# Exchanging the second and third of three matmuls per weight tile in a split-precision matrix product

## The reference, cut to what matters

```python
def sq_relu_mlp(h, w_in, w_out):
    return jnp.square(jax.nn.relu(h @ w_in)) @ w_out      # 2048 -> 8192 -> 2048

def conv_gated_mlp(h, w_up, conv_w, conv_b, w_down):
    up = h @ w_up                                          # 2048 -> 11264
    up = causal_depthwise_conv(up, conv_w) + conv_b
    gate, val = jnp.split(up, 2, axis=-1)
    return (jax.nn.silu(gate) * val) @ w_down              # 5632 -> 2048
```

## Time and profile before

| | |
|---|---|
| median of 3 runs | 2592.11 us (2591.83 to 2593.83) |
| the profiled execution | 2592.11 us, its span 2590.3 us |
| mean granted TensorE clock | 0.993 of full speed |
| TensorE matmul busy | 2537.2 us, 98% of the span |
| VectorE, ScalarE busy | 1658.1 us (64%), 1132.6 us (44%) |
| DMA | 547.89 MB, mean 212 GB/s |

### The profile page before, as it was taken

The page is one execution under the profiler, slowest core; times in us unless marked ns, Lnnn a source line. Parts: engine busy times, 40 slices in busy tenths (PEclk is TensorE's granted clock), DMA queues, the critical chain, the costliest instruction groups (busy, mean ns, idle before and its releaser), DMA issues.

```text
span 2590.3 us, 42561 instructions
## 1 busy us (share of the span) xinstructions
PE 2537.2 (98%) x18912; PEld 2378.3 (92%) x18912; DVE 1658.1 (64%) x1999; ACT 1132.6 (44%) x1299; POOL 11.2 (0%) x24
## 2 busy tenths in 40 slices
PE   6999999999999999999999999999999999999998
PEld 3688799999998999999999999999899889988996
DVE  5366666677785755555555579776677556764775
ACT  3322565544444434434434552054455435543553
POOL 0000000000000000000000000000000000000000
PEclk8999999999999999999999999999999999999999
DMA  9976565588885755555555555454455555555553
GB/s 395 361 254 229 209 218 207 202 296 290 304 292 202 278 190 186 194 192 185 194 193 184 190 183 179 147 179 170 151 185 196 196 194 187 188 195 184 190 183 110
DMA packets 77223, 547.89 MB, mean 212 GB/s; under 512 B 8848, under 2 KB 8976, under 8 KB 12272
## 3 DMA queue, kind: packets, MB, share of 16 engines
q1 hardware_dynamic: 74304, 533.53, 57.7%
q0 software_dynamic: 2448, 11.14, 1.1%
q10 hardware_dynamic: 288, 0.50, 0.1%
HBM read 539.90 MB, written 5.24 MB: 210 GB/s over the span
## 4 chain that ended last, share of the span: by engine, by line
PE 96%; DVE 2%; ACT 1%; DMA 1%; issue 0%; SPq 0%; DVEq 0%; ACTq 0%
PE acc L289 23%; PE acc L293 22%; PE acc L291 22%; PE acc L346 5%; PE acc L309 5%; PE acc L310 5%; PE acc L311 5%; PE mp L376 1%; PE mp L309 1%; PE mp L311 1%; PE mp L310 1%; DMA raw<-in_w_mod 1%; PE mp L435 0%; PE mp L498 0%; DVE macc L420 0%; PE mp L1866 0%
## 5 line engine op out<-in xcount | busy, mean ns | idle before, releaser
L257 DVE TENSOR_TENSOR wlo<-raw,whi 128x1024 fp32r<-128x1024 f32 x773 | 934.9, 1222 | 679.4 <-ACT whi L247 677.7
L247 ACT ACTIVATE whi<-raw 128x1024 fp32r<-128x1024 f32 x773 | 812.1, 1058 | 1171.9 <-PE acc L293 873.3
L293 PE MATMUL acc<-hl,whi 128*128 128x256 f32 x3296 | 922.6, 280 | 0.0
L289 PE MATMUL acc<-hh,whi 128*128 128x256 f32 x3296 | 919.4, 279 | 0.0
L291 PE MATMUL acc<-hh,wlo 128*128 128x256 f32 x3296 | 915.2, 278 | 0.0
L289 PEld LDWEIGHTS acc<-hh,whi 128*128 128x128 f32 x3296 | 622.5, 189 | 4.6 <-issue 3.0
L293 PEld LDWEIGHTS acc<-hl,whi 128*128 128x128 f32 x3296 | 618.8, 188 | 0.0
L291 PEld LDWEIGHTS acc<-hh,wlo 128*128 128x128 f32 x3296 | 616.7, 187 | 0.5
L293 PE MATMUL acc<-ml,whi 128*128 128x256 f32 x1536 | 430.1, 280 | 0.0
L289 PE MATMUL acc<-mh,whi 128*128 128x256 f32 x1536 | 426.4, 278 | 0.0
L291 PE MATMUL acc<-mh,wlo 128*128 128x256 f32 x1536 | 426.4, 278 | 0.0
(11 more groups left out here) (319 smaller groups left out, 2181.4 us busy)
## 6 DMA issues: line engine op xcount, KB each, us to landing
raw<-in_w_in SPq DMA_DIRECT2D x98, 1024.0 KB, 4.9
raw<-in_w_mod SPq DMA_DIRECT2D x96, 1024.0 KB, 5.8
raw<-in_w_up SPq DMA_DIRECT2D x88, 1024.0 KB, 4.9
raw<-in_w_mlp_in SPq DMA_DIRECT2D x64, 1024.0 KB, 4.9
raw<-in_w_mlp_out SPq DMA_DIRECT2D x64, 1024.0 KB, 4.9
raw<-in_w_down SPq DMA_DIRECT2D x44, 1024.0 KB, 4.9
raw<-in_w_out SPq DMA_DIRECT2D x32, 1024.0 KB, 4.9
raw<-in_w_fourier_out SPq DMA_DIRECT2D x8, 1024.0 KB, 5.7
```

The source lines that it names most:

```text
L247: nc.scalar.activation(whi[:, r, :], raw_slot(k)[:, 2 * GC * j:2 * GC * (j + 1)], ACT.Copy)\
L257: nc.vector.tensor_tensor(wlo[:, r, :], raw_slot(k)[:, 2 * GC * j:2 * GC * (j + 1)], whi[:, r, :].bitcast(f32), ALU.subtract).then_inc(S[" ...
L289: nc.tensor.matmul(dst, whi[:, r, cols], hi[:, kt, :], start=begin, stop=False, skip_group_check=True)
L293: last = nc.tensor.matmul(dst, whi[:, r, cols], lo[:, kt, :], start=False, stop=kt == nkt - 1, skip_group_check=True)
```

## The change

Within `feature_piece` the second and third matmul trade places. Before, the order is `whi` x high, `wlo` x high, `whi` x low; after it, `whi` x high, `whi` x low, `wlo` x high. The flag that closes the sum in PSUM and the increment of `used` stay with the third position. Operands, shapes, counts and waits are otherwise as before.

```diff
                     nc.tensor.matmul(dst, whi[:, r, cols], hi[:, kt, :], start=begin, stop=False,
                                      skip_group_check=True)
-                    nc.tensor.matmul(dst, wlo[:, r, cols], hi[:, kt, :], start=False, stop=False,
+                    nc.tensor.matmul(dst, whi[:, r, cols], lo[:, kt, :], start=False, stop=False,
                                      skip_group_check=True)
-                    last = nc.tensor.matmul(dst, whi[:, r, cols], lo[:, kt, :], start=False,
+                    last = nc.tensor.matmul(dst, wlo[:, r, cols], hi[:, kt, :], start=False,
                                             stop=kt == nkt - 1, skip_group_check=True)
```

## The result

The change made the kernel slower: 2611.32 us (2606.86 to 2614.71, 4 runs) against 2592.28 us for the kernel before, a ratio of 1.0067 with a 95% interval of 1.0055 to 1.0080. The profiled execution took 2611.55 us, its span 2609.7 us, 19.4 us more than before. Thirteen further executions of the changed kernel took 2605.1 to 2613.4 us, and no execution of the kernel before, in any session, took more than 2598.1 us. The time lies inside the stated range of 2570 to 2616 us, but the forecast was no change within 0.2%, and the kernel became 0.7% slower.

What follows compares the result with a forecast made beforehand. The prediction took TensorE's matmuls, busy 98% of the span, as the bound. Its sum was 2592.1 + 0 + 0 + 0 = 2592.1 us, no change within 0.2%, with a range of 2570 to 2616 us.

Steps and rivals of the forecast that it cites:

- (a): Later use of wlo in each feature_piece triple: no wait freed or added, place released at the same time; cost 0.
- (b): whi stationary twice in a row in feature_piece: the repeated load stays and overlaps the matmul ahead; cost 0.
- The 98 us: Most that could go over 15264 matmuls if the pitch fell 6.4 ns to the skill formula's 109.2 ns.
- Part (c): Sequence of gaps in feature_piece triples: the dear gap wanders, the sum stays 346.7 ns; bounds +23 and -25 us, value 0.
- The ring of members: Read across triples, both orders have the same cycle of weight loads, operand changes and PSUM target changes; 346.7 ns per triple.
- the dear gap: Longest gap in a triple, at its boundary from L293 to the next L289: 119 against 114 ns or so.
- the question the prediction left open: What sets the longest gap: change of PSUM target or tile, low activation, or load of whi after whi.
- Value taken: 0: Change in time put on the sequence of gaps over the 5088 triples of feature_piece: 0 us.
- an irregularity worth 1 us: Stretch from 521 to 571 us at 353.3 ns per triple instead of 346.7; 142 triples, 1 us.
- The second rival: feature_piece stays at the pace of 521 to 571 us, 353.3 ns per triple: 34 us at most, 2625 us; chance 0.07.
- The first rival: feature_piece slows to mm_lr's pace, all gaps about 117 ns, low activation in the middle: 2614 us; chance 0.13.
- Its other half: In feature_piece the pitch depends on how a weight load and the matmul streaming beside it meet; within the 0.13 rival.

Runs made afterwards that it cites:

- the third order: All triples as whi x low, whi x high, wlo x high, against the kernel before: 2609.91 us, ratio 1.0063.
- the tables: Separate small kernel of unbroken triple stretches, with byte offsets of weights and activations varied and several breaks ahead; paces from 113.33 to 123.6 ns per matmul.
- dl = 0: Small-kernel setting: low weights not shifted against the high ones (elements of 4 bytes; the kernel itself has dl = 16).
- pw = 36: Small-kernel setting: weights shifted 36 elements of 4 bytes against the activations (the kernel itself has 20).
- pw = 37: Small-kernel setting: weights shifted 37 elements of 4 bytes against the activations; 113.33 ns per matmul in all of its 16 stretches.

## Why the prediction was wrong

Its parts (a) and (b) held. No wait appeared or went, the supply still waits for TensorE, and the repeated `whi` tile is still loaded: 18912 loads. No load got cheaper: the gap beside a repeated `whi` tile is the same 119 ns as that beside a new one. The rule of the Trainium skill ("TensorE: Matmul & The Clock Gate", Part 2, step 1), that weights can be loaded once and used again, found nothing to act on here, since this stream issues a load with every matmul. The 98 us that the prediction worked out from a formula of the Trainium skill ("TensorE: Matmul & The Clock Gate", "Back-to-back issue gap") isn't a bound by that page: it gives the formula for an isolated matmul, and says that a stream of loads and matmuls keeps another spacing. The least pitch of any run here was 113.33 ns, above the formula's 109.2. The sum didn't use it.

Part (c) was half right. The ring of members does keep the sum inside a pace: 346.7 ns per triple at 1900 us in both orders, with the dear gap now behind the first matmul. That answers the question the prediction left open, since the load of `whi` after `whi` is what moved there.

The step that failed is the end of (c), "Value taken: 0", and behind it the sentence that a sum made of the same members stays 346.7 ns. The prediction had both paces in hand and read the dear one as an irregularity worth 1 us. The runs show that a triple at these offsets has two stable paces in either order, that what happens at the entry of a stretch picks one, and that a stretch can keep it for 600 us: 24 triples at the entries moved the time from 2611 to 2596 us, and 24 the other way from 2592 to 2619. The term that the sum put at 0 measured 19 us: the dear triples rose from some 380 to some 3070 of the 5088, and 2690 x 6.7 ns is 18 us.

The second rival was the mechanism that happened, at 0.07. Its argument against itself was wrong: that 1000 and 1900 us show the cheap pace "with quite different neighbours". What stands beside a stretch isn't what chooses. I had counted windows, where I should have counted entries: the windows from 930 to 1530 us are a single choice. Its price, 34 us at most, was right as a bound, because only part of the triples went dear. The first rival had the nearest number (2614 us), but its mechanism, the low activation in the middle, is refuted by the third order, which has it at the front and costs the same.

Its other half, that the meeting of a load and the matmul beside it sets the pitch, fits the tables, which show that the pitch depends on the operands' byte offsets, but isn't proved by them. Which part of the memory or of TensorE makes it so is open: no experiment here looked below the offsets. Open too is why the choice at a break falls as it does. Distances that differ by 2 to 5 ns went with different paces, so the changed kernel may well be cheap again after an unrelated edit.

## What to carry to other kernels

When TensorE is the bound and its stream is long, look at the pitch of matmuls and not at their duration, and compare it between stretches of the same code: two paces in one trace mean that the time hangs on more than the list of instructions. A small edit that moves such a kernel by under a per cent may have done so only by falling into another pace; test it with an edit at the entries before believing in it. The offsets of stationary and moving operands are worth a table: here moving `whi` by 92 bytes and `wlo` by 28 gave 1.5%, more than the edit under study, and a place is good only if all shapes and all breaks are good there.

## What the runs showed of the hardware that was not expected

- A stream of load and matmul pairs with 256 moving fp32r columns has several stable paces at one clock, among them 113.33, 115.56, 117.78, 120.0 and 123.33 ns per matmul. Which of them a stretch takes depends on the byte offsets and, where two are possible, on the entry. A pace once taken lasted through some 1770 triples, 627 us.
- Steps of 4 bytes between the operands' places change it: with dl = 0 and behind the float32 sum, 123.3 ns at pw = 36 and 113.33 at pw = 37.
- A float32r weight load of a tile that was just loaded isn't cheaper; the gap during which a `whi` tile follows a `whi` tile is the longest of the cheap pace, 119 ns against 113 and 114, in all six orders.
